# Mixture-of-experts block on one Trainium2 core: scatter-add into the output, with the down weights taken at every eighth column

## The reference, cut to what matters

```python
h = h + jnp.concatenate([conv_out, attn_out], axis=-1) @ w_o[l]
h = h + moe_ffn(rmsnorm(h, norm_ffn[l]), ...)

# inside moe_ffn, for the sorted (token, expert) pairs
gu = lax.ragged_dot(xs, w_gate_up, sizes) + b_gate_up[e_sorted]
gate = jnp.minimum(gu[:, :D_FF], SWIGLU_LIMIT)
up = jnp.clip(gu[:, D_FF:], -SWIGLU_LIMIT, SWIGLU_LIMIT)
act = (up + 1.0) * (gate * jax.nn.sigmoid(SWIGLU_ALPHA * gate))
out = lax.ragged_dot(act, w_down, sizes) + b_down[e_sorted]
out = out * gates.reshape(-1)[order][:, None]
y = jax.ops.segment_sum(out, token_of, num_segments=n_tok)
```

## Time and profile before

| | |
|---|---|
| median of 3 runs | 2206.23 us |
| the profiled execution | 2206.78 us |
| its span in the profile | 2205.0 us |
| granted PE clock, mean | 0.976 |
| PE busy | 2078.0 us (94%) |
| DVE, ACT, POOL busy | 738.2, 443.7, 563.1 us |
| DRAM read, written | 454.83 MB, 35.84 MB |

### The profile page before, as it was taken

One profiled execution on the slowest core, in us unless ns is written; L12 is line 12 of the kernel. 1 busy time (PEld: TensorE's weight loads), 2 busy tenths in 40 slices (PEclk: granted clock), 3 DMA queues, 4 the chain that ended last, 5 costly groups with the idle time before them and its releaser, 6 DMA issues.

```text
span 2205.0 us, 41908 instructions
## 1 busy us (share of the span) xinstructions
PE 2078.0 (94%) x15574; PEld 1883.0 (85%) x15575; DVE 738.2 (33%) x1949; ACT 443.7 (20%) x1078; POOL 563.1 (26%) x645
## 2 busy tenths in 40 slices
PE   7999999999968899999999999999999999999991
PEld 6777777745538899999999999999999999999991
DVE  1322333233443334234333333333233332343331
ACT  1333323232311111111111111111111111111110
POOL 2211111100233223322222322323223233232321
PEclk9999999999978999999999999999999999999996
DMA  7100000242517889999899999999999999999987
GB/s 251 40 10 11 10 11 1 80 131 47 145 39 228 268 281 310 313 297 304 270 305 277 310 289 298 310 284 289 301 312 318 308 272 283 321 315 319 306 284 88
DMA packets 305892, 486.97 MB, mean 221 GB/s; under 512 B 105920, under 2 KB 127200, under 8 KB 305792
## 3 DMA queue, kind: packets, MB, share of 16 engines
q1 hardware_dynamic: 247184, 437.28, 60.6%
q0 software_dynamic: 33376, 45.11, 9.9%
q10 hardware_dynamic: 25280, 3.85, 1.1%
HBM read 454.83 MB, written 35.84 MB: 223 GB/s over the span
## 4 chain that ended last, share of the span: by engine, by line
PE 91%; issue 2%; DVE 2%; ACT 1%; DMA 1%; POOL 1%; ACTq 0%; DVEq 0%; SPq 0%; POOLq 0%
PE psum L1003 43%; PE psum L1019 22%; PE psum L803 8%; PE psum L952 5%; PE psum L842 3%; PE psum L911 2%; PE psum L820 2%; PE psum L910 1%; PE psum L884 1%; PE psum L932 1%; PE psum L895 1%; DMA area<-in_w_in 1%; PE psum L982 1%; DVE area L1302 0%; DVE area L1297 0%
## 5 line engine op out<-in xcount | busy, mean ns | idle before, releaser
L1003 PE MATMUL psum<-area 128*128 128x128 f32 (+3 forms) x8192 | 980.2, 282 | 37.0 <-issue 18.9
L1003 PEld LDWEIGHTS psum<-area 128*128 128x128 f32 x8192 | 971.6, 192 | 42.4 <-issue 42.4
L1019 PE MATMUL psum<-area 128*128 128x128 f32 (+3 forms) x4096 | 496.4, 282 | 0.9
L1019 PEld LDWEIGHTS psum<-area 128*128 128x128 f32 x4096 | 484.5, 191 | 10.0 <-DVE area L1302 8.7
L1283 DVE TENSOR_SCALAR area<-psum,area 128x160 f32<-128x160 f32 x256 | 86.4, 380 | 615.6 <-PE psum L1003 615.6
L600 POOL DMA_INDIRECT sum_rows<-area x165 | 264.0, 1600 | 67.4 <-issue 40.2
L762 ACT ACTIVATE area<-area 128x320 f32<-128x320 f32 x128 | 60.4, 472 | 735.8 <-DVE area L1283 735.6
L803 PE MATMUL psum<-area 128*128 128x128 f32 x1536 | 176.8, 276 | 10.5 <-ACT area L681 4.0
L803 PEld LDWEIGHTS psum<-area 128*128 128x128 f32 x1536 | 173.3, 192 | 15.3 <-ACT area L677 5.8
L590 POOL DMA_INDIRECT area<-normed_rows,area x165 | 161.3, 977 | 61.5 <-issue 61.5
L585 POOL TENSOR_TENSOR area<-area 128x5 uint32<-128x5 uint32 x33 | 6.3, 190 | 617.4 <-DVE area L1268 590.4
(11 more groups left out here) (184 smaller groups left out, 1250.6 us busy)
## 6 DMA issues: line engine op xcount, KB each, us to landing
area<-in_w_gate_up SPq DMA_DIRECT2D x256, 1024.0 KB, 6.4
area<-in_w_down SPq DMA_DIRECT2D x128, 1024.0 KB
area<-in_w_in SPq DMA_DIRECT2D x3, 2048.0 KB, 21.5
area<-in_x SPq DMA_DIRECT2D x9, 512.0 KB, 4.0
area<-in_w_o SPq DMA_DIRECT2D x1, 4096.0 KB, 13.0
sum_rows<-area SPq DMA_DIRECT2D x32, 128.0 KB
normed_rows<-area SPq DMA_DIRECT2D x8, 512.0 KB, 3.1
out<-sum_rows SPq DMA_DIRECT2D x4, 1024.0 KB, 14.0
```

Of the source, the lines that this page charges most:

```text
L1003: ins = mm(dst, w_gu[piece][:, k, c * P:(c + 1) * P], xT[:, PART * s + k, 0:width], start=(s == 0 and k == 0 and c % 2 == 0), stop=(s == 1 ...
L1019: ins = mm(bank[4 + d // 3][:, (d % 3) * SLOTS:(d % 3) * SLOTS + width], w_dn[q][:, kk, d * P:(d + 1) * P], actT[:, 2 * q + kk, 0:width], ...
```

## The change

The scatters add into `out` itself, which now holds h from the start. For that each partition block must hold the columns 256 q to 256 q + 255, in their own order: output chunk d becomes the columns 8 p + d (p = 0 to 127) of the down weights and of the down bias, and the transpose back writes element n of chunk d at 8 n + d. The stationary operand of every down matmul is then read from SBUF with a step of 8 elements, 32 bytes. h is stored by one DMA for each block, in full rows. Scatter rows past the last token are dropped by a bounds check, and the zero fill for them goes, as do `sum_rows` and the last copy; SP waits for one signal from POOL instead.

```diff
-        acc_quarters = nc.dram_tensor("sum_rows", ((SEQ + SLOTS) * Q, QD), F32, kind="Internal").ap()
+        out_quarters = out[0].rearrange("t (q n) -> (t q) n", q=Q)
...
+        def output_chunk(ap, d):
+
+            return ap.rearrange("r (p k) -> r k p", k=KD)[:, d, :]
...
-                h_chunks = h_sb[b].rearrange("p (d q n) -> p d q n", d=KD, q=Q)
-                for q in range(Q):
-                    sp.dma_start(acc_by_chunk[i * P:(i + 1) * P, :, q, :], h_chunks[:, :, q, :]).then_inc(h_out, 16)
+                sp.dma_start(out[0][i * P:(i + 1) * P, :], h_sb[b]).then_inc(h_out, 16)
...
-                    sp.wait_ge(h_out, 16 * Q * (i + 1))
+                    sp.wait_ge(h_out, 16 * (i + 1))
...
-            sp.wait_ge(rows_free, n_tiles + 2)
-            out_chunks = out[0].rearrange("t (d q n) -> t d q n", d=KD, q=Q)
-            for q in range(Q):
-                sp.dma_start(out_chunks[:, :, q, :], acc_by_chunk[0:SEQ, :, q, :]).then_inc(final_out, 16)
-            sp.wait_ge(final_out, 16 * Q)
+            sp.wait_ge(all_added, 1)
...
-                    for dram in (hf_dram, acc_dram):
-                        pool.dma_start(dram[SEQ:SEQ + P, :], zeros).then_inc(zero_out, 16)
-                        pool.dma_start(dram[SEQ + P:, :], zeros[0:SLOTS - P, :]).then_inc(zero_out, 16)
+                    pool.dma_start(hf_dram[SEQ:SEQ + P, :], zeros).then_inc(zero_out, 16)
+                    pool.dma_start(hf_dram[SEQ + P:, :], zeros[0:SLOTS - P, :]).then_inc(zero_out, 16)
...
-                    g.indirect_dma_start(acc_quarters, bass.IndirectOffsetOnAxis(ap=put[:, k:k + 1], axis=0),
-                                         rows[:, k, :], None, compute_op=ALU.add).then_inc(scattered, 16)
+                    g.indirect_dma_start(out_quarters, bass.IndirectOffsetOnAxis(ap=put[:, k:k + 1], axis=0),
+                                         rows[:, k, :], None, compute_op=ALU.add, bounds_check=SEQ * Q - 1, oob_is_err=False).then_inc(scattered, 16)
...
+            pool.sem_inc(all_added, 1)
...
-                        ins = tr(bank[3][:, c * E:(c + 1) * E], bias_rows[0:E, 2 * FF + c * P:2 * FF + (c + 1) * P], ident[0:E, 0:E])
+                        ins = tr(bank[3][:, c * E:(c + 1) * E], output_chunk(bias_rows[0:E, 2 * FF:], c), ident[0:E, 0:E])
...
-                                 w_dn[q][:, kk, d * P:(d + 1) * P], actT[:, 2 * q + kk, 0:width],
+                                 output_chunk(w_dn[q][:, kk, :], d), actT[:, 2 * q + kk, 0:width],
...
-                    V.transpose(rows[:, k, :].rearrange("p (d n) -> p d n", d=KD),
+                    V.transpose(rows[:, k, :].rearrange("p (n d) -> p d n", d=KD),
                                 outT[:, :, 32 * k:32 * k + 32]).then_inc(rows_turned, 1)
```

More of the change, by code:

```diff
@@ L344, in build @@
         hf_quarters = nc.dram_tensor("normed_rows", ((SEQ + SLOTS) * Q, QD), F32, kind="Internal").ap()
-        acc_quarters = nc.dram_tensor("sum_rows", ((SEQ + SLOTS) * Q, QD), F32, kind="Internal").ap()
+        out_quarters = out[0].rearrange("t (q n) -> (t q) n", q=Q)
         lists = nc.dram_tensor("token_lists", (LISTED, 2), U32, kind="Internal").ap()
-        hf_dram, acc_dram = (a.rearrange("(t q) n -> t (q n)", q=Q) for a in (hf_quarters, acc_quarters))
-        acc_by_chunk = acc_quarters.rearrange("(t q) (d n) -> t d q n", q=Q, d=KD)
+        hf_dram = hf_quarters.rearrange("(t q) n -> t (q n)", q=Q)
+        def output_chunk(ap, d):
+            return ap.rearrange("r (p k) -> r k p", k=KD)[:, d, :]
         x_rows = I["x"][0].rearrange("(t p) n -> t p n", p=P)
@@ L381, in build @@
         rt_done, lg_read, top_ready, e_ready, mask_ready = (sem(n) for n in ("rt_done", "lg_read", "top_ready", "e_ready", "mask_ready"))
-        zero_ready, zero_out = sem("zero_ready"), sem("zero_out")
+        zero_ready, zero_out, all_added = sem("zero_ready"), sem("zero_out"), sem("all_added")
         pool_passed = sem("pool_passed")
@@ L394, in build @@
         down_done, outT_ready = sem("down_done"), sem("outT_ready")
-        rows_turned, rows_ready, rows_free, scattered, final_out = (sem(n) for n in ("rows_turned", "rows_ready", "rows_free", "scattered", "final_out"))
+        rows_turned, rows_ready, rows_free, scattered = (sem(n) for n in ("rows_turned", "rows_ready", "rows_free", "scattered"))
         block = ctx.enter_context(nc.Block())
@@ L577, in _ @@
             wait(tables_ready, 1)
-            wait(zero_out, 16 * 4)
+            wait(zero_out, 16 * 2)
             pool.sem_inc(rows_free, 1)
@@ L605, in _ @@
             n_tiles = pool.value_load(n_i[0:1, 0:1], min_val=1, max_val=MAX_TILES)
-            wait(h_out, 16 * Q * NT)
+            wait(h_out, 16 * NT)
             wait(hf_out, 16 * NT)
@@ L1159, in _ @@
                     if n == HEADS - 1:
-                        dve.wait_ge(zero_out, 16 * 4)
+                        dve.wait_ge(zero_out, 16 * 2)
                     dve.wait_ge(pv_done, n + 1)
@@ L1221, in _ @@
             dve.wait_ge(hf_out, 16 * NT)
-            dve.wait_ge(h_out, 16 * Q * NT)
+            dve.wait_ge(h_out, 16 * NT)
             ch.link(V.tensor_copy(count, bank[6][:, 0:E]))
```

## The result

The change makes the kernel slower: 2664.48 us median of 4 runs (2663.1 to 2669.94) beside 2206.99 us for the kernel before. The ratio is 1.207, with a 95% interval of 1.2055 to 1.2086: +457 us. The sign was forecast, the size was not: 2563 us, with an upper end of 2605.

What follows compares the result with a forecast made beforehand. PE's matmul pitch was taken to bound the tiles, with a bare last copy as tail. The sum was 2206.8 - 26 + 1 + 396 - 15 = 2563 us, own range 2525 to 2605, or 2178 to 2605 with the free-load rival.

Steps and rivals of the forecast that it cites:

- (1): End of the span: the last copy of 27.2 us goes, about 1 us stays behind the scatters, -26 us.
- (5): Transposes back on DVE: strided writes cost +196 ns each, hidden inside tiles, +1 us in the tail.
- (2): Stores of h: three of four per block go, already hidden by PE's queue, 0; 3.7 us at most.
- (3): Zero fill of the spare rows, two early DMAs on POOL: nobody waits there, 0.
- (4): Scatters on POOL: a bounds check may lengthen each, hidden inside tiles; -2 to +3 us, taken as 0.
- Rival C: DVE becomes the bound through costly strided writes: 2211 us; chance 0.05 together with whatever else ends near today's time.
- (6): Down weight loads on PE: strided reads raise the pitch to 217 ns at every width, +396 us (+367 to +424).
- (7): PE's weight waits in two early tiles and slower stages behind them vanish as down slows: -15 us (0 to -20).
- A: Down weight load: the stride is free on PE, 2182 us (2178 to 2186); chance 0.35.
- B: Down weight loads: overlap partly hides the penalty, pitch 140 to 190 ns, 2350 us; chance 0.06.
- D: Down stages: slow loads and PE's clock falls to half after each, 2717 us; chance 0.04.

Runs made afterwards that it cites:

- the dense run: The changed kernel with only the down matmuls reading their weights in contiguous blocks of 128 columns again: 2192.81 us beside 2209.00, ratio 0.993.
- run 16: Not a run number: 16 is the gain in us of the dense run, the changed kernel with contiguous down weights, 2192.81 us beside 2209.00.
- the first two experiments: Changed kernel with down weights read in contiguous blocks again: 2192.81 us; kernel before with down matmuls reading every eighth column of the weights: 2681.37 us.

## Why the prediction was right or wrong

- **(1) the last copy, -26 us: wrong by 7.** With (5)'s 1 us I had -25 for the end of the span. The profiles give -18 from PE's last matmul on, and the dense run 16 in all. The step that failed is "SP's pass and the end of the program, which I put at 1 us": behind the copy lay 3 us of POOL's empty loop turns and a DRAIN of 5.6 us. The run with the last scatter outside the loops took 5 us of this away. The DRAIN's row was in the trace before, at 2181.7 us; I had not asked what else the copy covered.
- **(2) and (3), the stores of h and the zero fill, 0: right.** The chain reaches the first tile at 671.38 us in place of 671.85. A gain or loss of a few us would not be seen there, since other runs with the same stores reach it at 674.04 and 677.04 (last scatter outside, dense weights).
- **(4) the scatters, 0: right.** 1605 ns with the bounds check, 1600 without.
- **(5) the transpose back, +196 ns for each: right.** 629 ns in place of 412, +217, and DVE still idles 0.84 us before line 1294 (1.61 before). Rival C never came near.
- **(6) the weight loads, 217 ns, bounds 210 and 224: the step that failed.** No free slack and no dependence on the width, as argued; but 242 ns, outside both bounds: 64 x 64 x 25 ns = 102 us, as much as the whole miss of 2563 against 2664. I took what a step *adds* on DVE, 0.77 ns for each element, and added it to PE's load. What the runs show is a time for each new line: 1.8 to 1.9 ns on PE at steps 2, 3, 4 and 8, as weight or as moving operand, with about the same result for 64, 96 and 128 lines. PE reads a dense element in 0.9 ns, and by the difference of these two it loses 1.0 ns where DVE loses 0.8. "Twice the load" was no bound either; I had no row for it.
- **(7) hidden weight waits, -15 us: -21, near by luck.** In the places that I named it gave 6 us: the two long stalls keep 2 us each, and the stages behind them stay slow (17.89 and 16.18 us). The rest came from what I had left out, the short waits at 13 other tile starts and faster matmuls behind them (up to 1.3 us for one gate stage, wait and matmuls together).
- **Rivals.** A (free load) falls by the first two experiments; B (part of the penalty vanishes in the overlap) falls, since pieces are fully 242 ns a matmul; D (lower clock) falls: the mean granted clock is 0.984 in place of 0.976, and gate and up pieces are as before. My argument against D misread its row, though: the earlier trace rows has a slice of 7 tenths from 606 to 661 us, and of the router's steps the one at 616.58 us takes 3.62 us for 16 matmuls where the earlier trace rows has 1.79.

With 242 ns for (6), which is +498, -18 for (1), -21 for (7) and 0 for (5), whose tail is in the 18, the sum of the prediction gives 2666. That is no test of its own, for the terms come from the same profile. The two errors beside (6) were +7 and -6 us and nearly cancel.

## What to carry to other kernels

When the inner step of an operand in SBUF leaves less than two float32 elements in each 16-byte line, each line costs 1.8 to 1.9 ns at steps of 3, 4 and 8 elements and 1.7 to 2.1 at the others, in PE's weights and, as far as tried (step 8), in its moving operand too. A matmul hides such a load only when it is wide (136 ns for 160 columns make 242 ns for some 285, an estimate). Put the permutation on an engine that waits (here 16 transposes on DVE behind idle time), not in the operand of the engine that bounds the kernel. And before a tail is counted as gained, list what runs beneath it: loop exits and the end-of-program DRAIN come to light when it goes.

## What the runs showed of the hardware that was not expected

- Where one operand is strided, the distance in time between matmuls follows the number of its 16-byte lines: 64 lines 113 to 122 ns, 96 lines 174, 128 lines 219 to 242 (but see step 12), 160 lines 289. No run has both operands strided.
- Among steps that all touch a new line each time, 12 elements (48 bytes) take 268 ns and 16 elements (64 bytes) 219. It follows the step and not the first column. The cause is open.
- POOL's DRAIN at the end of the program took 5587 ns before and after the change, and in the two kernels where SP waited for the transfers instead its end still lies 5.7 us behind POOL's last issue.
- DVE transposes 32 x 32 blocks from one partition quarter into another, 32 partitions by 320 elements in a median of 503 ns.
